# A two-model layer stack on one core: the recurrent mixer's scores built by levels, and every engine's order set anew

## The reference

```python
def step(state, inp):
    qc, kc, vc, lfc = inp
    cum = jnp.cumsum(lfc, axis=2)
    last = cum[:, :, -1:, :]
    qd = qc * jnp.exp(cum)
    kd = kc * jnp.exp(-cum)
    scores = jnp.where(causal, jnp.einsum('bhtk,bhsk->bhts', qd, kd), 0.0)
    o = (jnp.einsum('bhts,bhsv->bhtv', scores, vc)
         + jnp.einsum('bhtk,bhkv->bhtv', qd, state))
    new_state = (jnp.exp(last[:, :, 0, :])[..., None] * state
                 + jnp.einsum('bhsk,bhsv->bhkv', kc * jnp.exp(last - cum), vc))
    return new_state, o
```

```python
hid = jnp.einsum('cd,ced->ce', xc, jnp.take(u, ec, axis=0)).astype(jnp.float32)
w = (gc * jax.nn.gelu(hid, approximate=False)).astype(xc.dtype)
return jnp.einsum('ce,ced->cd', w, jnp.take(v, ec, axis=0))
```

## Time and profile before

| what | us |
|---|---|
| median of 3 runs | 2318.24 |
| lowest and highest run | 2311.13, 2322.93 |
| span of the profiled execution, first to last instruction | 2204.1 |
| what lies around the span, by the median | 114.1 |
| PE busy, DVE busy | 1852.7, 1473.0 |
| POOL busy, ACT busy | 1124.4, 726.2 |
| read from HBM | 770.80 MB |

### The profile page before, as it was taken

How to read it: one execution, slowest core, us unless ns; L and a number is a source line. 1 busy time by engine, 2 the same in 40 slices (tenths; PEclk the granted TensorE clock), 3 DMA queues, 4 the chain that set the end, 5 groups by cost and what they waited for, 6 DMA issues and landing times.

```text
span 2204.1 us, 28240 instructions
## 1 busy us (share of the span) xinstructions
PE 1852.7 (84%) x10240; PEld 1223.7 (56%) x10240; DVE 1473.0 (67%) x3734; ACT 726.2 (33%) x1882; POOL 1124.4 (51%) x1028
## 2 busy tenths in 40 slices
PE   6999886689897687898677999877299988999998
PEld 3798575457544173545125565431166655567786
DVE  1388688855658776457896356587868778567564
ACT  3466123345422111321021153102025533346363
POOL 0000035575767676677776577676775667640000
PEclk8999897798898899999898999988689999999999
DMA  9999868799999999999999999999999999995360
GB/s 391 376 407 362 318 250 307 268 385 363 407 379 337 406 363 406 395 373 406 389 405 409 399 397 375 406 368 389 366 394 401 363 374 360 356 409 201 134 243 26
DMA packets 213459, 774.85 MB, mean 352 GB/s; under 512 B 23868, under 2 KB 24776, under 8 KB 213320
## 3 DMA queue, kind: packets, MB, share of 16 engines
q0 software_dynamic: 147456, 536.94, 63.5%
q1 hardware_dynamic: 65864, 236.11, 27.4%
HBM read 770.80 MB, written 2.16 MB: 351 GB/s over the span
## 4 chain that ended last, share of the span: by engine, by line
PE 39%; POOL 20%; DMA 18%; DVE 13%; issue 7%; ACT 2%; SPq 0%; DVEq 0%; ACTq 0%; POOLq 0%
POOL gat L1475 20%; PE ps L717 15%; DMA gat<-in_peer_v_dram,idxv 8%; DMA gat<-in_peer_u_dram,idx 7%; PE ps L1582 5%; DVE gat L1494 4%; PE ps L1235 3%; PE ps L1650 2%; PE ps L1013 2%; PE ps L1033 2%; PE ps L2723 1%; DVE ws L2108 1%; DVE ws L2106 1%; PE ps L821 1%; DMA wbuf<-in_win_dram 1%
## 5 line engine op out<-in xcount | busy, mean ns | idle before, releaser
L1494 DVE CUSTOM_DVE_ANT_0 gat<-gat,X 128x1024 f32<-128x1024 f32 x512 | 615.3, 1222 | 311.3 <-DMA gat<-in_peer_u_dram,idx 306.6
L1475 POOL DMA_INDIRECT gat<-in_peer_u_dram,idx x512 | 571.0, 1115 | 470.0 <-DVE ws L1327 292.2
L1475 POOL DMA_INDIRECT gat<-in_peer_v_dram,idxv x512 | 553.2, 1080 | 388.0 <-PE ps L1582 198.9
L717 PE MATMUL ps<-hn,wbuf 128*128 128x256 f32 (+1 forms) x2976 | 593.5, 357 | 38.6 <-DVE ws L1152 10.9
L717 PEld LDWEIGHTS ps<-hn,wbuf 128*128 128x128 f32 x2976 | 505.2, 197 | 124.6 <-issue 40.5
L1582 PE MATMUL ps<-gat,spread 128*32 128x512 f32 x2048 | 426.9, 656 | 113.0 <-DMA gat<-in_peer_v_dram,idxv 98.6
L1582 PEld LDWEIGHTS ps<-gat,spread 128*32 128x32 f32 x2048 | 81.8, 115 | 381.9 <-DMA gat<-in_peer_v_dram,idxv 227.8
L1235 PE MATMUL ps<-wbuf,oT 128*128 128x512 f32 x208 | 94.7, 609 | 2.7 <-DVE oT L1211 2.3
L1102 ACT ACTIVATE ws<-ws 128x16 f32<-128x16 f32 (+6 forms) x224 | 77.2, 347 | 35.0 <-DVE ws L1169 28.8
L861 DVE CUSTOM_DVE_ANT_0 gat<-gat,row 128x1024 f32<-128x1024 f32 x64 | 76.1, 1219 | 8.4 <-DMA gat<-in_ada_dram 4.3
L717 PE MATMUL ps<-ws,wbuf 128*128 128x256 f32 x256 | 61.9, 407 | 15.3 <-DVE ws L960 15.3
(11 more groups left out here) (373 smaller groups left out, 2599.1 us busy)
## 6 DMA issues: line engine op xcount, KB each, us to landing
wbuf<-in_win_dram SPq DMA_DIRECT2D x160, 512.0 KB, 8.3
gat<-in_ada_dram SPq DMA_DIRECT2D x120, 512.0 KB, 12.4
wbuf<-in_wout_dram SPq DMA_DIRECT2D x34, 512.0 KB, 6.5
wbuf<-in_pq_dram SPq DMA_DIRECT2D x32, 512.0 KB, 8.5
wbuf<-in_kvw_dram SPq DMA_DIRECT2D x32, 512.0 KB, 8.7
gat<-in_kvada_dram SPq DMA_DIRECT2D x16, 512.0 KB, 14.4
gat<-in_peer_u_dram,idx POOLq DMA_INDIRECT x512, 7.5
gat<-in_peer_v_dram,idxv POOLq DMA_INDIRECT x512, 7.8
```

What stands on the lines that cost most here:

```text
L717: i = e.do.matmul(psum, wview(name, g, kc // 2, turn)[:, kc % 2, m * P:m * P + P], src[:, kc, :], start=kc == 0, stop=kc == KC - 1)
L1475: e.do.indirect_dma_start(gat[g][:, :], None, t["peer_" + kind], bass.IndirectOffsetOnAxis(at, 0)).then_inc(*ldg[g].put(kind, l, b, *unit))
L1494: e.do.tensor_tensor_reduce(g[:, :], g[:, :], X[b % 2][:, :], 1.0, 0.0, ALU.mult, ALU.add, hid[:, e_ // 16 % 2, e_ % 16:e_ % 16 + 1]).then ...
```

## The change

**The mixer.** The seven scalings in a row and the seven panels of 128 columns go. Decays are now made from sums of logarithms: two scans of eight numbers on DVE (new L1191), six small subtractions (L1194 to L1200), and one exponential on ACT. The scores are made in levels. Within 16 tokens, one full product as before (L1062). Between two neighbouring groups of 16, four products of 16x16 (L1065). Between neighbouring groups of 32, two products of 32x32 (L1069), and between the halves one of 64x64 (L1072). All of them write one 128x128 square of PSUM. DVE scales the keys and queries for the levels (L1218 to L1228: a 128x256 product, four of 128x128, and two of 128x256). The upper triangle is copied at once by DVE with a new mask `upto` (L1241). ACT copies the transposed keys alone, and for the last block nothing. The buffers are now one set per head parity.

**The order.** `LATE` is replaced by `PLAN`, a table of due times for all engines, POOL too, and the order of weight loads is a list of its own, `LOADS`. `PLAN` moves steps of all stages. Three places follow. A matmul's line number in the changed kernel is larger: L1062 to L1075 are the mixer's scores, L1634 is the expert quad (before L1582), L749 the projections (L717), L1973 the norm of stage E (L1921), L978 the norm of the other stages (L946), L1342 and L1591 the turns of weights (L1290, L1539).

The diff, cut to its core:

```diff
-CONSTS = ["ident", "ones", "cols", "strict", "nones", "mask16", "ntri", "reset", "negm", "iota", "fold", "range"]
+CONSTS = ["ident", "ones", "cols", "strict", "nones", "upto", "ntri", "reset", "negm", "iota", "fold", "range"]
...
-    c["mask16"] = same(16) & (i <= j)
+    c["upto"] = i <= j
...
-def weave(late, *parts):
+def weave(at, *parts):
...
-        return t + late[n][step] if n < len(late) and step < len(late[n]) else t
+        return at[n][step] if n < len(at) and step < len(at[n]) else t
...
-    hset = [{k: tA(3, TM) if k == "sg" else tA(2, P) if k == "v" else tA(TM)
-             for k in ("sg", "kk", "cum", "ecum", "kd", "dl", "qd", "v", "sq", "o1")} for _ in range(2)]
-    kset = [{"KM": wide(tA, at_A, 1024, 1152), "qP": tA(P), "sc": tA(P), "KT": tA(P), "pre": tA(16)} for _ in range(2)]
+    hset = [{k: tA(3, TM) if k == "sg" else tA(2, P) if k in ("v", "sc", "KT") else tA(TM)
+             for k in ("sg", "kk", "cum", "ecum", "kd", "dl", "qd", "v", "sq", "o1", "sc", "KT")} for _ in range(2)]
+    for q in hset:
+        q["decay"] = tA(80)
+        q["k32"], q["q32"], q["k64"], q["q64"] = tA(4, 2, 16), tA(4, 2, 16), tA(2, 4, 16), tA(2, 4, 16)
...
-    LATE = [
...
+    LOADS = [
+        ("win", 1, 0), ("win", 0, 0), ("win", 2, 0), ("win", 3, 0), ("win", 4, 0), ("win", 5, 0), ("win", 6, 0), ("win", 7, 0), ("wout", 0, 0),
...
+    PLAN = {
+        "PE": [
...
-        loads.extend(sorted((when, key) for key, when in first.items()))
+        loads.extend(sorted(((when, key) for key, when in first.items()),
+                            key=lambda load: (LOADS.index((*load[1][:2], load[1][3])), load)))
...
-            for r in range(1, 8):
-                e.wait_ge(*(hgA.at("km", H, j, r - 1) if r > 1 else hgV.at("km", H, j)))
-                e.do.matmul(ps[:, B, 16 * r:16 * r + 16], KM[:, (r - 1) * P:r * P], q["qd"][:, j * P + 16 * r:j * P + 16 * r + 16],
+            e.do.matmul(ps[:, B, 0:P], q["kd"][:, sl], q["qd"][:, sl], start=True, stop=True)
+            e.wait_ge(*hgV.at("k16", H))
+            for r in range(0, P, 32):
+                e.do.matmul(ps[r:r + 16, B, r + 16:r + 32], k16[:, at + r:at + r + 16], q["qd"][:, at + r + 16:at + r + 32],
                             start=True, stop=True)
-            e.wait_ge(*hgV.at("kd", H))
-            e.do.matmul(ps[:, B, P:2 * P], q["kd"][:, sl], q["qd"][:, sl], start=True, stop=True)
-            e.wait_ge(*hgA.at("km", H, j, 7))
-            e.do.transpose(ps[:, B, 2 * P:3 * P], KM[:, 7 * P:8 * P], C["ident"]).then_inc(*hgP.put("m3", H, j))
+            e.wait_ge(*hgV.at("q32", H))
+            for r in range(2):
+                e.do.matmul(ps[64 * r:64 * r + 32, B, 64 * r + 32:64 * r + 64], q["k32"][:, 2 * j + r, :, :], q["q32"][:, 2 * j + r, :, :],
+                            start=True, stop=True)
+            e.wait_ge(*hgV.at("q64", H))
+            i = e.do.matmul(ps[0:64, B, 64:P], q["k64"][:, j, :, :], q["q64"][:, j, :, :], start=True, stop=True)
+            if b < NB - 1:
+                e.wait_ge(*hgV.at("k128", H))
+                i = e.do.transpose(ps[:, B, P:2 * P], k128[:, sl], C["ident"])
+            i.then_inc(*hgP.put("m3", H, j))
...
-                e.wait_ge(*hgV.at("qp", H, j))
-                i = e.do.matmul(ps[:, O, sl], SA[:, hh, :], qP, start=False, stop=True)
+                e.wait_ge(*hgV.at("qp", H))
+                i = e.do.matmul(ps[:, O, sl], SA[:, hh, :], qP[:, sl], start=False, stop=True)
...
+            for j in range(2):
+                if 2 * before[0] + j < NB - 1:
+                    e.wait_ge(*hgP.at("kv", before, j))
...
+        yield when + 6.6
+        e.wait_ge(*hgV.at("decay", H))
+        e.do.activation(q["decay"], q["decay"], ACT.Exp).then_inc(*hgA.put("decay", H))
...
-        for j in range(2):
-            KM = kset[j]["KM"]
-            ed = q["ecum"][:, j * P:(j + 1) * P].rearrange("p (n c) -> p n c", c=16)[:, :, 15]
-            yield when + 10.4 + 2.2 * j
-            e.wait_ge(*hgV.at("km", H, j))
-            for r in range(1, 8):
-                if r > 1:
-                    e.wait_ge(*hgA.now())
-                e.do.activation(KM[:, r * P:r * P + 16 * r], KM[:, (r - 1) * P:(r - 1) * P + 16 * r], ACT.Identity,
-                                scale=ed[:, r:r + 1]).then_inc(*hgA.put("km", H, j, r))
...
-            z = kset[j]
+            if 2 * c + j == NB - 1:
...
-            e.wait_ge(*hgP.at("m3", H, j))
...
-            e.do.activation(z["sc"][:, 16:P], ps[:, B, 16:P], ACT.Identity).then_inc(*hgA.put("sc", H, j))
-            e.do.activation(z["KT"], ps[:, B, 2 * P:3 * P], ACT.Identity).then_inc(*hgA.put("KT", H, j))
+            e.wait_ge(*hgV.at("sc", H, j))
+            e.do.activation(q["KT"][:, j, :], ps[:, bankM.of("hg", "s", H, j), P:2 * P], ACT.Identity).then_inc(*hgA.put("KT", H, j))
...
+        sums, k128w, qPw, k64w, q64w, k32w, q32w = (q["decay"][:, lo:lo + n] for lo, n in
+                                                    ((0, 16), (16, 16), (32, 16), (48, 8), (56, 8), (64, 8), (72, 8)))
...
+        if (c, hh) >= (0, 2):
+            before = head_two_before(c, hh)
+            for j in range(2):
+                if 2 * before[0] + j < NB - 1:
+                    e.wait_ge(*hgV.at("st", 2 * before[0] + j, before[1]))
+        for j in range(2):
+            i = e.do.tensor_tensor_scan(sums[:, 8 * j:8 * j + 8], C["ones"][:, 0:8], c16[:, 8 * j:8 * j + 8, 15], 0.0, ALU.mult, ALU.add)
+            i.then_inc(*hgV.put("sums", H, j))
+        e.wait_ge(*hgV.now())
+        e.do.tensor_tensor(qPw, sums, c16[:, :, 15], ALU.subtract).then_inc(*hgV.put("qpw", H))
+        e.do.tensor_tensor(halves(k128w), bc(halves(sums)[:, :, 7:8], 2, 8), halves(sums), ALU.subtract).then_inc(*hgV.put("k128w", H))
+        e.do.tensor_tensor(four(k64w), bc(halves(sums)[:, :, 3:4], 2, 4), halves(sums)[:, :, 0:4], ALU.subtract).then_inc(*hgV.put("k64w", H))
+        e.do.tensor_tensor(two(k32w), bc(groups(sums)[:, :, 1:2], 4, 2), groups(sums)[:, :, 0:2], ALU.subtract).then_inc(*hgV.put("k32w", H))
+        e.wait_ge(*hgV.at("qpw", H))
+        e.do.tensor_tensor(four(q64w), halves(qPw)[:, :, 4:8], bc(halves(sums)[:, :, 3:4], 2, 4), ALU.subtract).then_inc(*hgV.put("q64w", H))
+        e.do.tensor_tensor(two(q32w), groups(qPw)[:, :, 2:4], bc(groups(sums)[:, :, 1:2], 4, 2), ALU.subtract).then_inc(*hgV.put("decay", H))
...
-            e.wait_ge(*hgA.at("kk", H))
-            if (c, hh) == (0, 0):
-                e.wait_ge(*hgV.at("pre0", j))
-            else:
-                e.wait_ge(*hgP.at("m3", before, j))
-            e.do.tensor_tensor(KM.rearrange("p (r c) -> p r c", c=144)[:, :, 0:16], q["dl"][:, sl].rearrange("p (r c) -> p r c", c=16),
...
-            e.do.tensor_tensor_scan(pre[:, 1:9], ed, C["ones"][:, 0:8], 1.0, ALU.mult, ALU.mult).then_inc(*hgV.put("pre", H, j))
...
-            e.do.tensor_tensor(z["qP"].rearrange("p (n c) -> p n c", c=16), q["qd"][:, sl].rearrange("p (n c) -> p n c", c=16),
...
+        k16 = q["kk"]
+        e.do.tensor_tensor(k16, q["dl"], q["kk"], ALU.mult).then_inc(*hgV.put("k16", H))
+        e.wait_ge(*hgA.at("decay", H))
+        e.wait_ge(*hgV.now())
+        e.do.tensor_tensor(q["k32"], by16(k16, 4)[:, :, 0:2, :], bc(w16(k32w, 2), 4, 2, 16), ALU.mult).then_inc(*hgV.put("k32", H))
+        e.do.tensor_tensor(q["q32"], by16(q["qd"], 4)[:, :, 2:4, :], bc(w16(q32w, 2), 4, 2, 16), ALU.mult).then_inc(*hgV.put("q32", H))
+        yield when + 12.2
+        e.do.tensor_tensor(q["k64"], by16(k16, 8)[:, :, 0:4, :], bc(w16(k64w, 4), 2, 4, 16), ALU.mult).then_inc(*hgV.put("k64", H))
+        e.do.tensor_tensor(q["q64"], by16(q["qd"], 8)[:, :, 4:8, :], bc(w16(q64w, 4), 2, 4, 16), ALU.mult).then_inc(*hgV.put("q64", H))
+        e.do.tensor_tensor(q["dl"].rearrange("p (n c) -> p n c", c=16), k16.rearrange("p (n c) -> p n c", c=16),
+                           bc(k128w.rearrange("p (n c) -> p n c", c=1), 16, 16), ALU.mult).then_inc(*hgV.put("k128", H))
+        e.do.tensor_tensor(q["cum"].rearrange("p (n c) -> p n c", c=16), q["qd"].rearrange("p (n c) -> p n c", c=16),
+                           bc(qPw.rearrange("p (n c) -> p n c", c=1), 16, 16), ALU.mult).then_inc(*hgV.put("qp", H))
...
-            e.wait_ge(*hgA.at("KT", H, j))
-            e.do.copy_predicated(z["sc"], C["mask16"].bitcast(U32), ps[:, B, P:2 * P]).then_inc(*hgV.put("sc", H, j))
+            e.wait_ge(*hgP.at("m3", H, j))
+            if (c, hh) < (0, 2):
+                e.wait_ge(*hgV.at("sc0", hh))
+            e.do.copy_predicated(q["sc"][:, j, :], C["upto"].bitcast(U32), ps[:, B, 0:P]).then_inc(*hgV.put("sc", H, j))
...
-                i = e.do.scalar_tensor_tensor(SA[:, hh, :], SA[:, hh, :], z["pre"][:, 8:9], ps[:, B, 3 * P:4 * P], ALU.mult, ALU.add)
+                i = e.do.scalar_tensor_tensor(SA[:, hh, :], SA[:, hh, :], sums[:, 8 * j + 7:8 * j + 8], ps[:, B, 2 * P:3 * P], ALU.mult, ALU.add)
...
-        weave([], *[pool_experts(e, l, c) for l in range(2) for c in range(2)])
```

(3 more changed lines are left out.)

74 lines of the change are left out of this document (35 added, 39 removed), and 426 rows, old and new, of tables (LATE, LOADS, PLAN).

## The result

The change makes the kernel slower. The median of after is 2333.3 us (2319.0 to 2352.1, 20 runs), that of before beside it 2316.6 us (2300.1 to 2335.1, 20 runs). The ratio is 1.0075, with a 95% interval of 1.0055 to 1.0096. I had forecast 2251 us, with a range of 2215 to 2292. The runs of this document were taken in groups, each with runs of before beside it; the medians of before and all ratios leave out the runs in which the chip was in its slower state.

The account below looks back on a forecast made before the run. PE was taken to bound the start and the tail, transfers most of the gathers. Terms of -13 (start), -13 (gap), +11 (tiles) and -52 (tail) made -67 us: 2251 us against 2318.24, range 2215 to 2292.

Parts of the forecast that it names:

- Work on PE that lies beside the saturated gathers costs nothing as long as it fits: Gather phase: extra PE work is free while transfers are the bound and PE has room; cost 0.
- I take it as fitting, at no cost on PE: Before the last quad: the 58 us of PE work moved out of the tail fit beside the gathers.
- Slower: the quads get stuck: Rival, gathers: quads behind stage E pieces free buffers 0.9 us later each, 115 us added, 2366 us; chance 0.04.
- the cover does not hold: Rival, after 1825 us: only 17 us free take up the moved 58, quads end 41 us later, 2292 us; chance 0.16.
- A set of narrow products: 0.76 us forecast: Mixer's scores on PE: a set takes 0.76 us instead of 1.95, saving 19 us in each chunk.
- The start: -13 forecast: Ahead of the first gather: the mixer on chunk 0 ends earlier, 13 us gained, bounds 0 and 19.
- It is covered there by PE: First window: DVE's 18 us more work a chunk hides behind PE; uncovered, DVE is late by at most 18 us.
- From 293 to 450: -13 forecast: After the first gather: six quads ahead of chunk 1's scores fill DMA, 13 us gained, bounds 0 and 27.
- The tail: -52 forecast: Behind the last quad: 191 fewer instructions, 58 us less PE work, tail 152 us instead of 204.
- the 22 us for 71 instructions of many kinds: Tail: the remaining 71 of the 191 removed instructions, priced like L2427, make 22 of the 58 us.
- The 114.1 us around the span stay.: Outside the traced span: 114.1 us of measured time remain, added to the forecast span of 2137 us.
- The 11 us for the moved weight tiles: Saturated gathers: 8 moved weight tiles, 4.2 MB at 377 GB/s, add 11 us, bounds 0 and 11.

Follow-up runs that it names:

- p3: New mixer in the order of before up to planning clock 1790, the new order after that: 2214.9 us, 0.9998 times before.
- a3_after: The changed kernel, unedited, run again in a group where before takes 2213.9 us: span 2244.2 us.
- half quads: 14 of each block's 16 quads multiply 256 columns instead of 512: on the changed kernel 2219.1 us (1.0026), on new mixer with old order 2198.4 us (0.9932).
- p5: New mixer in the order of before, with the new order only from planning clock 1160 to 1480: 2226.3 us, 1.0054 times before.
- p6: Changed kernel with the order of before from planning clock 1160 to 1480, and weight tiles loaded in order of first use: 2281.7 us, 1.0299 times before.
- h3_old_order: New mixer with the order of before for all engines, gathers and weight loads: 2204.1 us, 0.9968 times before.
- s1: New mixer in the order of before, with the new order only from planning clock 38 to 270: 2292.4 us, 0.9930 times before.
- c2: New mixer in the order of before, with the second half of every top-16 search left out (output wrong): 2286.0 us, 0.9902 times before.
- b0_before: The kernel before, unedited, run again for a trace: 2212.7 us, span 2210.7 us.

## Why the prediction was wrong, step by step

**"Work on PE that lies beside the saturated gathers costs nothing as long as it fits."** This is the step that failed, and with it "I take it as fitting, at no cost on PE". I compared sums: 58 us of work against 17 us free behind 1825 us, 227 before and 19 from the mixer. p3 shows the price at the place itself: 43 us gained in the tail, 53 lost ahead of it, PE about as busy as in the old order (161 to 159 us of 180). With the transfers saturated, what counted here was not PE's free time but when each quad freed its buffers. The rival "Slower: the quads get stuck" named just this, with its point of decision: "0.52 us a quad". In `a3_after` POOL waited 95 us longer for quads than in the old order, 0.75 us for each of 128. The milder rival, "the cover does not hold", had quads 41 us later from the pulled work alone, where p3 shows 53 to 60. The harsher mechanism was seen and given 0.04, because I argued from where the moved work was put and not from how long a quad waits there.

**The order of the rest.** The prediction had no term for it. It treated the new order as a set of pieces moved, while all steps were moved. The half quads show that 38 of the 100 us between the orders are PE's work standing ahead of quads. For the other 60 the traces show PE idle from 750 to 1260 and overfull behind it, and p5 shows that one stretch of 320 us is worth 16 us. By POOL's waits 45 of the 60 are again waits for quads, and 24 are longer instructions of POOL's own. What in the order makes the quads late is not shown piece by piece, and p6 warns against adding pieces.

**A set of narrow products: 0.76 us forecast.** Right in kind, and too dear. PE in order of time, in `h3_old_order`:

```profile
144.37 0.24 PE L1464 MATMUL ps<-ws 128*16 128x16 f32 x8
144.43 0.24 PE L1468 MATMUL ps<-ws 128*32 128x32 f32 x4
144.60 0.33 PE L1471 MATMUL ps<-ws 128*64 128x64 f32 x2
144.86 0.33 PE L1474 MATMUL ps<-cst,ws 128*128 128x128 f32 x1
```

From the first strip to the transpose behind the set are 0.49 us, against 1.95 before, and the four strips are inside 0.3 us as forecast. The products that change the form start 0.06, 0.17 and 0.26 us behind the ones ahead, each before these have ended by the trace, whose ends of matmuls are modelled. The rule of the Trainium skill ("TensorEngine Tiling (Array Packing)", Tiling Modes), that a change of the mode drains TensorE, is not borne out here either: the three changes together lie inside 0.49 us.

**The start: -13 forecast, 0 to -3 measured.** The mixer's own gain, 19 us, is there (188.4 to 169.4), at the upper bound of 19. But only with the new order: in the old one PE waits for DVE's operands (16 us in 9 waits) and 2 us remain. Of what takes it back outside the mixer, the late first norm is shown (13 us); the dots ahead of the search stand in the chain of s1, and their share was not measured apart. The prediction read only what the mixer removes, and not what the new order puts ahead of it: of the step "It is covered there by PE" the cover is gone as soon as PE is faster. The output projection starts at 226.2 instead of the forecast 219; in s1 at 217.0.

**From 293 to 450: -13 forecast.** Gather 64 comes at 416 us instead of 433 in the traces of one group, 17 earlier, so this gain came. But gather 384 is back at 956 against 959: it did not last until then.

**The tail: -52 forecast, -43 measured.** The mechanism was right, and one term was too large. PE's busy time in the tail, before in the first row and `a3_after` in the second:

```profile
2005.00:2210.00 205.00, 191.21 (x1359) 159.33 (x1351) 115.88 (x327) 101.64 (x307) 0.00 (x0) 0.98 0.38 138
```

```profile
2085.00:2244.00 159.00, 145.38 (x975) 118.08 (x974) 88.26 (x238) 76.53 (x223) 0.00 (x0) 0.96 0.39 140
```

46 us went, not 58. The term with the weakest ground was the 22 us for 71 instructions of many kinds, priced like L2427; if the other terms hold it came to about 10, which was not measured apart. PE's idle time is 13.6 us, where I had let it grow to 20. Block 2's norm runs at 1885.8 us, 195 us ahead of the last quad instead of 80, and costs PE a wait of 22 us for ACT:

```profile
L1973 PE MATMUL ps<-dgn,h 128*128 128x128 f32 x64 | 9.5, 307 | 22.3 <-ACT dgn L1936 22.3
```

**"The 114.1 us around the span stay."** Wrong as told: time and span differ by 2 us in every run. It did not move the forecast, which is 67 us under the median by either reading. But it hid that the trace of before was from another condition than its times. In that other condition after loses 17 us to before, where it loses 30 to 34 us in the condition of the first trace. Why is open, for before has no trace in it; c2, with the old order, has a DMA share of 0.95 between 293 and 1970 us there, where `h3_old_order` has 0.98.

The 11 us for the moved weight tiles were not measured apart; they are within the gather phase. Between the traces of `b0_before` and `a3_after` the sum is then: start -3 where I had -13, gather phase +80 where I had -2, tail -43 where I had -52.

## What to carry to other kernels

Where transfers are saturated and their buffers are freed by an in-order engine, work moved ahead of the end must be priced by the delay of each release, not by the idle time of the engine: 53 us of gathers were lost here for 43 us of tail. Before a trace is subtracted from a time, the two must be from the same condition: here a time 114 us above its span meant another execution, not overhead.

## What the runs showed that was not expected

The same program takes 2214 to 2216 us in some groups and 2307 to 2324 us in others, and one chip gave both. With the longer times the gathers' queue is no fuller but emptier, and the chain holds something that the profile doesn't place ("another core or an unknown queue", 3 to 7% of the chain, absent in the traces with the shorter times). The queue of the gathers in `h3_old_order`, `a3_after` and c2 (packets, MB, share of 16 engines' span):

```profile
q0 software_dynamic: 147456, 536.94, 63.7%
```

```profile
q0 software_dynamic: 147456, 536.94, 63.5%
```

```profile
q0 software_dynamic: 147456, 536.94, 62.5%
```

With the spans of 2196.2, 2244.2 and 2287.6 us this is 151.8, 154.6 and 155.1 ns a packet. So each gathered row is 2.8 ns dearer with the new order as well, 26 us over the queue, in one group (`h3_old_order` and `a3_after`), where the two kernels differ only in their orders. Why rows get dearer when they are issued at other times is not shown.
